# Hybrid decoder step on one core: the final sum and norm moved into the experts' block, with the sample tile on GpSimd

## The reference

```python
f = hier_moe(u, ...)                 # each token: gate0 * expert_a(u) + gate1 * expert_b(u)
hp = hp + f[:B * S].reshape(B, S, D) # prompt rows, 256 x 2048
hs = hs + f[B * S:].reshape(DB, DS, D)  # sample rows, 8 x 2048
y_prompt = rms_norm(hp, norm_final_g)
y_sample = rms_norm(hs, norm_final_g)
# rms_norm(x, g) = x * rsqrt(mean(x * x) + 1e-6) * g, all in float32
```

## Time and profile before

| | |
|---|---|
| median of 3 runs | 1697.02 us (1693.51 to 1700.8) |
| the profiled execution's own time | 1693.25 us |
| its span, first to last instruction | 1691.5 us |
| busy: PE, DVE, ACT, GpSimd | 77%, 40%, 14%, 4% |
| mean granted clock of TensorE | 0.864 |
| mean rate of the DMAs | 341 GB/s |

### The profile page before, as it was taken

The page is one execution under the profiler, slowest core; times in us unless marked ns, Lnnn a source line. Parts: engine busy times, 40 slices in busy tenths (PEclk is TensorE's granted clock), DMA queues, the critical chain, the costliest instruction groups (busy, mean ns, idle before and its releaser), DMA issues. The chain is left out here.

```text
span 1691.5 us, 24894 instructions
## 1 busy us (share of the span) xinstructions
PE 1299.3 (77%) x7991; PEld 816.7 (48%) x7992; DVE 678.5 (40%) x4789; ACT 230.3 (14%) x447; POOL 60.7 (4%) x100
## 2 busy tenths in 40 slices
PE   5999487888697979379997676676777577876771
PEld 3777355555465756237774222443444344433431
DVE  3005875756575757677446950020010000000015
ACT  1011011301212203020002111010011001100101
POOL 1000000000000000010000000000001000000000
PEclk9999789998898989679998767687899878888995
DMA  8453899999989999999997999959999999999954
GB/s 269 90 191 141 286 389 394 398 398 391 354 335 398 370 398 356 373 362 335 362 359 298 408 389 364 404 226 384 395 360 396 393 377 383 357 389 392 393 222 156
DMA packets 201805, 576.59 MB, mean 341 GB/s; under 512 B 28529, under 2 KB 116898, under 8 KB 183618
## 3 DMA queue, kind: packets, MB, share of 16 engines
q1 hardware_dynamic: 122144, 507.85, 76.8%
q10 hardware_dynamic: 75122, 58.46, 10.8%
q0 software_dynamic: 4432, 9.05, 1.7%
HBM read 568.68 MB, written 17.77 MB: 347 GB/s over the span
## 5 line engine op out<-in xcount | busy, mean ns | idle before, releaser
L119 DVE CUSTOM_DVE_ANT_0 ws<-ws,xgT 128x128 f32<-128x128 f32 x2048 | 441.8, 282 | 68.2 <-DMA ws<-in_cache_fox_k 29.4
L1682 PE MATMUL bank<-ws,xgT 128*64 128x256 f32 x1024 | 264.2, 423 | 127.5 <-DMA ws<-in_w_expert_up 123.9
L800 PE MATMUL bank<-xn,ws 128*128 128x264 f32 x1024 | 266.1, 417 | 53.3 <-DMA ws<-in_w_in 53.3
L800 PEld LDWEIGHTS bank<-xn,ws 128*128 128x128 f32 x1024 | 204.0, 205 | 140.2 <-DMA ws<-in_w_in 61.0
L1682 PEld LDWEIGHTS bank<-ws,xgT 128*64 128x64 f32 x1024 | 154.2, 154 | 236.0 <-DMA ws<-in_w_expert_up 121.1
L1684 PE MATMUL bank<-ws,xgT 128*64 128x256 f32 x1024 | 264.1, 423 | 0.0
L785 PE MATMUL bank<-ws,PR 128*32 128x512 f32 x1024 | 155.4, 688 | 35.5 <-DMA ws<-in_cache_fox_v 28.5
L1839 DVE COPY gu<-bank 128x256 f32<-128x256 f32 x32 | 13.6, 425 | 412.6 <-PE bank L1684 412.6
L119 DVE DVE_READ_ACCUMULATOR2_ANT Z<- 128x1 f32 x2048 | 159.6, 78 | 0.0
L1684 PEld LDWEIGHTS bank<-ws,xgT 128*64 128x64 f32 x1024 | 154.1, 154 | 0.0
L1703 PE MATMUL bank<-ws,hT 128*32 128x512 f32 x1024 | 115.9, 605 | 12.7 <-ACT xgT L1757 12.5
(11 more groups left out here) (372 smaller groups left out, 954.7 us busy)
## 6 DMA issues: line engine op xcount, KB each, us to landing
ws<-in_cache_sb_k SPq DMA_DIRECT2D x128, 512.0 KB, 8.2
ws<-in_cache_fox_k SPq DMA_DIRECT2D x128, 512.0 KB, 10.0
ws<-in_cache_sb_v SPq DMA_DIRECT2D x128, 512.0 KB, 7.2
ws<-in_cache_fox_v SPq DMA_DIRECT2D x128, 512.0 KB, 10.2
ws<-in_w_expert_gate SPq DMA_DIRECT2D x32, 2048.0 KB, 15.4
ws<-in_w_expert_up SPq DMA_DIRECT2D x32, 2048.0 KB, 17.3
ws<-in_w_expert_down SPq DMA_DIRECT2D x32, 2048.0 KB, 20.0
ws<-in_w_in ACTq DMA_DIRECT2D x16, 2048.0 KB, 31.7
```

The source lines that it names most:

```text
L119: ins = dve.tensor_tensor_reduce(k, k, qb[:, (g * H + h) * HD:(g * H + h + 1) * HD], 1.0, 0.0, ALU.mult, ALU.add, Z[:, n % 2, g, h, t:t + 1])
L800: mm = pe.matmul(out[:, 0:T], w[:, c, m * P:(m + 1) * P], xn[:, c, :], start=(c == 0), stop=(c == KC - 1))
L1682: pe.matmul(bank[2 * k][0:SLOTS, 0:256], lhs, ws[:, wg, c * 256:(c + 1) * 256], start=(c == 0), stop=(c == KC - 1))
```

## The change

The second block is gone; its instructions stand behind the experts' in the same block. What differs beside the place:

- GpSimd loads the five register values before the pairs instead of after them, and signals `all` when the last scatter has landed and the five branches are behind it. SP waits for `all`, then issues the six loads in the same order. It stores the tiles in the order 0, 2, 1.
- PE turns the residual rows in the last pair, between `gate_up(0)` and `gate_up(1)` (`token_rows`), through banks 4 to 7, and waits for all twelve copies before `down(0)`. ACT copies the banks to SBUF (`hrow`, which lies in `qo` and `xn`), before the last pair's Silu.
- The sample tile (2) is summed and normed on GpSimd, in single operations of 8x2048: `tensor_scalar` and `tensor_tensor` where DVE had one fused operation. Its reciprocal alone is on DVE, its square and root on ACT.
- DVE has the two prompt tiles, with one 128x2048 operation where there were four of 128x512, and its first addend comes from SBUF, not from a bank. Its order is add 0, add 1, reciprocal of tile 2, norm 0, norm 1. ACT's order is tile 2, 0, 1.

The diff, cut to its core; the second block's old text is left out, since it stands above:

```diff
+    hrow = [qo[:, :, :].rearrange("p c t -> p (c t)")[:, t * D:(t + 1) * D] for t in range(2)]
+    hrow.append(xn[:, :, :].rearrange("p c t -> p (c t)")[:, D:2 * D])
...
         @block.sync
...
             extra_pairs(sp, pair)
+            sp.wait_ge(F["all"], 1)
+            for t in (2, 0, 1):
+                lo, n = TILES[t]
+                for k in range(2):
+                    sp.dma_start(yr[0:n, t, k, :], y_rows[k * T + lo:k * T + lo + n, :]).then_inc(F[f"g{t}{k}"], 16)
+            for t in (0, 2, 1):
+                lo, n = TILES[t]
+                sp.wait_ge(F[f"out{t}"], 1)
+                dst = y_prompt[0, lo:lo + n] if t < 2 else y_sample.rearrange("b s d -> (b s) d")
+                sp.dma_start(dst, hr[0:n, t, :]).then_inc(F["st"], 16)
+            sp.wait_ge(F["st"], 48)
...
         @block.gpsimd
...
+            used = [in_use(pool, 2 * i) for i in range(PAIRS - EXP_PAIRS)]
             pool.wait_ge(E["dst"], 1)
...
             for n in range(EXP_PAIRS, PAIRS):
-                with pool.If(in_use(pool, 2 * (n - EXP_PAIRS)) > 0):
+                with pool.If(used[n - EXP_PAIRS] > 0):
...
+            pool.memset(pad[:, 7:8], 0.0).then_inc(F["all"], 1)
+            own = Steps(pool, F["pool"])
+            out, y0, y1 = hr[0:NB, 2, :], yr[0:NB, 2, 0, :], yr[0:NB, 2, 1, :]
+            pool.wait_ge(F["hc"], 12)
+            pool.wait_ge(F["g20"], 16)
+            own.step(pool.tensor_scalar(y0, y0, gates[0:NB, 2, 0:1], None, ALU.mult))
+            own.step(pool.tensor_tensor(out, y0, hrow[2][0:NB, :], ALU.add))
+            pool.wait_ge(F["g21"], 16)
+            own.step(pool.tensor_scalar(y1, y1, gates[0:NB, 2, 1:2], None, ALU.mult))
+            pool.tensor_tensor(out, out, y1, ALU.add).then_inc(F["sum2"], 1)
+            pool.wait_ge(F["sq2"], 1)
+            pool.tensor_scalar(rms[0:NB, 2:3], ssq[0:NB, 2:3], 1.0 / D, EPS, ALU.mult, ALU.add).then_inc(F["ms2"], 1)
+            pool.wait_ge(E["gf"], 16)
+            own.step(pool.tensor_tensor(out, out, gf[0:NB, :], ALU.mult))
+            pool.wait_ge(F["rec2"], 1)
+            pool.tensor_scalar(out, out, ssq[0:NB, 2:3], None, ALU.mult).then_inc(F["out2"], 1)
...
         @block.tensor
...
+            def token_rows():
+                pe.wait_ge(E["yc0"], 2 * EXP_PAIRS - 2)
+                pe.wait_ge(E["yc1"], 2 * EXP_PAIRS - 2)
+                for i in range(12):
+                    lo, n = TILES[i // 4]
+                    if i >= 4:
+                        pe.wait_ge(F["hc"], i - 3)
+                    for c in range(4):
+                        mm = pe.transpose(bank[4 + i % 4][0:n, c * P:(c + 1) * P], xT[:, 4 * (i % 4) + c, lo:lo + n], ident[:, :])
+                    mm.then_inc(F["hp"], 1)
...
-            def pair(n, ahead, first=False):
+            def pair(n, ahead, first=False, last=False):
                 pe.wait_ge(E["xgT"], 4 * n + 4)
                 gate_up(0, n)
+                if last:
+                    token_rows()
...
+                if last:
+                    pe.wait_ge(F["hc"], 12)
                 down(0, n)
                 down(1, n)
...
         @block.scalar
...
+            def token_rows():
+                for i in range(12):
+                    t, k = divmod(i, 4)
+                    n = TILES[t][1]
+                    act.wait_ge(F["hp"], i + 1)
+                    nc.scalar.activation(hrow[t][0:n, k * 512:(k + 1) * 512], bank[4 + k][0:n, :], ACT.Copy).then_inc(F["hc"], 1)
...
+            def pair(n, ahead, last=False):
+                if last:
+                    token_rows()
                 silu(0, n)
...
+            for t in (2, 0, 1):
+                n = TILES[t][1]
+                act.wait_ge(F[f"sum{t}"], 1)
+                if t != 2:
+                    act.wait_ge(F["sq2" if t == 0 else "sq0"], 1)
+                nc.scalar.activation(junk[0:n, :], hr[0:n, t, :], ACT.Square, accum_out=ssq[0:n, t:t + 1]).then_inc(F[f"sq{t}"], 1)
+                act.wait_ge(F[f"ms{t}"], 1)
+                nc.scalar.activation(rms[0:n, t:t + 1], rms[0:n, t:t + 1], ACT.Sqrt).then_inc(F[f"sqrt{t}"], 1)
...
         @block.vector
...
+            def add(t):
+                dve.wait_ge(F[f"g{t}0"], 16)
+                dve.wait_ge(F["hc"], 4 * t + 4)
+                fin.step(dve.scalar_tensor_tensor(out=hr[:, t, :], in0=yr[:, t, 0, :], scalar=gates[:, t, 0:1],
+                                                  in1=hrow[t], op0=ALU.mult, op1=ALU.add))
+                dve.wait_ge(F[f"g{t}1"], 16)
+                dve.scalar_tensor_tensor(out=hr[:, t, :], in0=yr[:, t, 1, :], scalar=gates[:, t, 1:2],
+                                         in1=hr[:, t, :], op0=ALU.mult, op1=ALU.add).then_inc(F[f"sum{t}"], 1)
...
+            add(0)
+            add(1)
+            dve.wait_ge(F["sqrt2"], 1)
+            dve.reciprocal(ssq[0:NB, 2:3], rms[0:NB, 2:3]).then_inc(F["rec2"], 1)
+            norm(0)
+            norm(1)
```

More of the change, by code:

```diff
@@ L521, in hybrid_step @@
         bctx.close()
-        experts(nc, ctx, ws, W, a, ident, iota, gcol, lastq, xT, xn, xgT, xg, wr, br, bank, sem, E, idx, dest, gates, extra,
+        experts(nc, ctx, ws, W, a, ident, iota, gcol, lastq, xT, xn, qo, xgT, xg, wr, br, bank, sem, E, idx, dest, gates, extra,
                 many, many2, destc, drow, sqs, srs, y_prompt, y_sample, u_rows, y_rows)
@@ L1554, in attention_and_route, with experts @@
         bstack.close()
-def experts(nc, ctx, ws, W, a, ident, iota, gcol, lastq, xT, xn, xgT, xg, wr, br, bank, sem, E, idx, dest, gates, extra,
+def experts(nc, ctx, ws, W, a, ident, iota, gcol, lastq, xT, xn, qo, xgT, xg, wr, br, bank, sem, E, idx, dest, gates, extra,
             many, many2, destc, drow, sqs, srs, y_prompt, y_sample, u_rows, y_rows):
@@ L1563, in experts @@
     gf = sb("gf", [P, D])
+    ssq = sb("ssq", [P, 3])
+    rms = sb("rms", [P, 3])
     dctx = ExitStack()
@@ L1579, in experts @@
     EXP_PAIRS = NE // 2
+    hrow = [qo[:, :, :].rearrange("p c t -> p (c t)")[:, t * D:(t + 1) * D] for t in range(2)]
+    hrow.append(xn[:, :, :].rearrange("p c t -> p (c t)")[:, D:2 * D])
+    rows = ws[:, :, :].rearrange("p s (a d) -> p (s a) d", d=D)
+    hr = rows[:, 0:3, :]
+    yr = rows[:, 3:9, :].rearrange("p (t k) d -> p t k d", k=2)
+    junk = rows[:, 9, :]
+    F = {n: sem("e_" + n) for n in ("hp hc all g20 g21 g00 g01 g10 g11 sum0 sum1 sum2 sq0 sq1 sq2 ms0 ms1 ms2 "
+                                    "sqrt0 sqrt1 sqrt2 rec2 out0 out1 out2 st dve pool").split()}
     def in_use(eng, i):
@@ L1747, in _ @@
                 pair(n, True)
-            pair(EXP_PAIRS - 1, False)
+            pair(EXP_PAIRS - 1, False, last=True)
             extra_pairs(pe, lone_pair)
@@ L1765, in silu @@
                 nc.scalar.activation(si[k][:, :, :], gv[:, :, 0:SLOTS], ACT.Silu).then_inc(E[f"si{k}"], 1)
-            def pair(n, ahead):
+            def token_rows():
[7 more added lines that the diff above has]
+                    token_rows()
                 silu(0, n)
@@ L1786, in _ @@
                 pair(n, True)
-            pair(EXP_PAIRS - 1, False)
+            pair(EXP_PAIRS - 1, False, True)
             extra_pairs(act, lone_pair)
+            for t in (2, 0, 1):
[6 more added lines that the diff above has]
+                nc.scalar.activation(rms[0:n, t:t + 1], rms[0:n, t:t + 1], ACT.Sqrt).then_inc(F[f"sqrt{t}"], 1)
         @block.vector
@@ L1855, in _ @@
             extra_pairs(dve, pair)
-    dctx.close()
[L1859 to L1941, removed]
@@ new lines, in _ @@
+            fin = Steps(dve, F["dve"])
+            def add(t):
[6 more added lines that the diff above has]
+                                         in1=hr[:, t, :], op0=ALU.mult, op1=ALU.add).then_inc(F[f"sum{t}"], 1)
@@ new lines, in norm @@
+            def norm(t):
+                dve.wait_ge(F[f"sq{t}"], 1)
+                dve.tensor_scalar(rms[:, t:t + 1], ssq[:, t:t + 1], 1.0 / D, EPS, ALU.mult, ALU.add).then_inc(F[f"ms{t}"], 1)
+                dve.wait_ge(F[f"sqrt{t}"], 1)
+                fin.step(dve.reciprocal(ssq[:, t:t + 1], rms[:, t:t + 1]))
+                dve.wait_ge(E["gf"], 16)
+                dve.scalar_tensor_tensor(out=hr[:, t, :], in0=hr[:, t, :], scalar=ssq[:, t:t + 1],
+                                         in1=gf[:, :], op0=ALU.mult, op1=ALU.mult).then_inc(F[f"out{t}"], 1)
```

## The result

The change made the kernel slower by a little: 1699.13 us in the median (20 runs, 1694.48 to 1704.36) against 1693.26 us for the kernel before (20 runs, 1685.04 to 1700.8) measured beside it. The medians differ by 5.9 us; the ratio is 1.0036 [1.0024, 1.0048], which is 4.1 to 8.1 us. Predicted were +2.6 us, 1695.8 us on the profiled execution; that execution of after took 1699.14 us, span 1697.4 us. The range held the result, but the loss is 5.9 us in place of 2.6.

What follows compares the result with a forecast made beforehand. The bound was DVE's 23.7 us tail after the first load, plus 4.3 us for the last store. Loads 6.95 us earlier, but GpSimd-DVE waits move DVE's end from 1687.2 to 1689.8: 1693.25 + 2.6 = 1695.8 us, range 1685.5 to 1704.

Steps and rivals of the forecast that it cites:

- The front: Before the tail's loads: one block drops drain and barrier, register loads move early; first load issues 6.95 us earlier.
- Rival E: Before the tail's loads: the 3.83 us drain stands ahead of `all` too; 1699.6 us, chance 0.06.
- The rows in the last pair: Residual transposes and copies fit under PE's 9.21 us wait for the up weights; effect zero, 5.1 us if uncovered.
- The clock: At gate_up(1) of the last pair: PE kept warm would save 1.45 us; taken as 0, kept for the range.
- The exclusion: In the tail: GpSimd operations reading SBUF and DVE products with two SBUF inputs each wait for the whole other.
- A: Main case, tail: GpSimd and DVE exclude each other; +2.6 us, 1695.8 us, chance 0.46.
- B: Rival, tail: same GpSimd durations, but side by side with DVE; -4.7 us, 1688.5 us, chance 0.27.
- The tensor_tensor: GpSimd's 8x2048 add in the sample tile takes 4.90 us, one input at cast pace, the second at memset pace.
- tensor_scalar: 0.33 + 1.72 = 2.05 to 0.33 + 2.85 = 3.18 ... so I take 2.05: GpSimd's 2048-column scale in the sample tile, from memset and cast paces; taken at the lower end, 2.05 us.
- Rival D: Tail: GpSimd at the cast's pace, 3.18 and 6.03 us, excluding DVE; +9.4 us, 1702.6 us, chance 0.11.
- the prediction's chain through ACT, the gain and norms 0 and 1: Tail after the sample's sum at 1674.4: ACT's squares and roots, GpSimd's gf product, DVE's norms, to 1689.8.
- the prediction's lower end for the gain: Before the tail's loads: gain 3.83 us less if GpSimd has the drain's delay anyway after its last indirect transfer.

Runs made afterwards that it cites:

- experiment 8: Changed kernel with sample tile back on DVE, its norm and store last, and register loads again behind the last scatter; one execution 1689.72 us against 1692.21 before.
- experiment 3: Kernel before, plus six GpSimd operations on spare data at the start of the experts' block, where GpSimd is free; one execution, 1692.75 us.
- experiment 5: Kernel before, plus six GpSimd 8x2048 sums on spare data in its second block, nobody waiting for them; one execution, 1705.63 us.
- experiment 2: Changed kernel with the sample tile's final sum and norm left out, its output rows zero; 1681.74 us, ratio 0.9949.
- experiment 4: Changed kernel with GpSimd's scales written as tensor_tensor, the factor broadcast over the columns; 1696.85 us, ratio 1.0038.

## Why the prediction came out as it did

**The front: right.** Predicted 6.95 us, measured 6.77; both of its halves stand in experiment 8. Rival E, the drain ahead of `all` too, is out.

**The rows in the last pair: right at zero.** PE's transposes run from 1618.75 to 1624.2 and ACT's copies to 1625.3, under the wait for the up weights, which ends at 1627.93. From the last pair's `gate_up(0)` to the memset of `pad` the trace has 38.56 us before and 38.68 after. The clock was not kept: gate_up(1) again starts at 0.50, as in the earlier trace rows, after 3.73 us in which PE did nothing. One stage of after (us, PE, PEld, DVE, ACT and POOL busy, granted clock, DMA share, GB/s):

```profile
1628.00:1630.90 2.90, 2.90 (x14) 1.85 (x16) 0.00 (x0) 0.00 (x0) 0.00 (x0) 0.50 0.89 373
```

**The exclusion: right**, and it was the choice between A and B: experiments 3 and 5 show it from both sides, with 8 partitions. The Trainium skill's sentence (SBUF — State Buffer, SBUF: two separate sides) that this is an exclusive lock, taken for the whole instruction, agrees with these rows for the adds. For a tensor_scalar it does not: DVE's product ran in its last 1.9 us.

**The tensor_tensor: nearly right.** Taken at 4.90 us, it is 4.50 alone in experiment 3; the Trainium skill's 4497 ns (GPSIMD Engine Reference, Elementwise — side-by-side cycle accounting) is that number.

**The step that failed is "tensor_scalar: 0.33 + 1.72 = 2.05 to 0.33 + 2.85 = 3.18 ... so I take 2.05".** It is 5.45 us, outside both ends, and was drawn from a memset and a cast: neither does arithmetic with a factor, and the ends were one kind of guess twice, not bounds. The working had one input cheaper than two; here the tensor_scalar with its one tensor (5.45) is dearer than the add of two (4.50), though a copy of one is cheap (1.90). Why is open. Against the predicted steps, from the first load:

| step | predicted | measured |
|---|---|---|
| GpSimd's start | 2.9 | 3.19 |
| scale y0 | 2.05 | 5.45 |
| add | 4.90 | 4.68 |
| DVE product, then scale y1 | 2.2 + 1.8 | 7.36, of which 1.9 wait |
| DVE product | 2.2 | none: beside the scale's end |
| add | 4.7 | 4.68 |
| sum of the sample | 20.8 | 25.6 |
| DVE's last end | 36.2 | 40.4 |

The scales' excess of 2 x 3.4 us came back in part, 2.2 us, since a DVE product fits beside the end of a tensor_scalar; with the small differences of the other rows 4.8 us are left at the sample's sum. From there the prediction's chain through ACT, the gain and norms 0 and 1 took 14.8 us against 15.4, in the order that it names; the last scale (7.35 us, from 1684.16) held DVE's norm 1 for 2.8 us. The span's end comes 5.4 us after DVE's, not 4.3: the stores of the sample and of tile 1 are ready within 0.4 us, where the prediction had 2.9 and more. Whether that is its cause stays open, since experiment 2 has 5.28 us with its last store 2.9 us behind the one before, and experiment 4 has 4.29 with 2.1 us between its last two. So +2.6 became 2.6 + 0.2 + 4.2 + 1.1 = 8.1 us in these two traces. Rival D, +9.4, came nearest to these traces, and that is luck: it made the adds dear (6.03), which they are not, and the scales 3.18.

**Two points on the sum itself.** Its terms are smaller than the sizes stated for them: a product of 2.35 us is put in as 2.2 and the second and third scale of 2.05 as 1.8, without a reason. With the stated sizes and 0.1 us a handover the same chain ends at about 1692.5, which is +5.3: nearer to the result, and for the wrong reason. The traces bear out the 2.2: a product held by an add ended 2.15 us behind it (1677.17 to 1679.32). And 1699.6 us, the sum on the median of three runs, lies 0.5 us from the 1699.13 measured only because that median was 3.8 us above the one of 20 runs, while the loss was 3.3 us too small.

## What to carry to other kernels

Before work is given to GpSimd to relieve DVE, ask what DVE reads meanwhile: beside GpSimd arithmetic, products with both inputs in SBUF stop, and those with a bank as an input don't. Ask also who waits for GpSimd's result: here ACT's queue did, and the prompt tiles behind it. Both together made 18.5 us of a sample tile that was 4.0 us on DVE. An operation that the trace doesn't have is not bounded by cheaper kinds of operation; its range must reach at least to the dearest operation whose price is known, and what the kernel's time would be is worked out at that end too. What paid here, in the traces: no block boundary ahead of a chain of loads and register values loaded early (6.8 us), DVE's longer operations with the new order (0.9), and the smallest store last (1.4), which together take 9.1 us off the tail.

## What the runs showed that was not expected

- On GpSimd, 2048 columns of f32: tensor_scalar 5.45 us, tensor_tensor 4.50 and copy 1.90 (experiment 3), tensor_tensor with a broadcast factor 3.59 (experiment 4), memset 1.79 (experiment 2) to 1.81. The number of partitions changes nothing (5.45 and 5.48).
- A tensor_scalar of 5.45 us holds DVE's products for 3.4 to 3.6 us of them, a tensor_tensor to its end. Waits go both ways: beside DVE products of 2.35 us, a tensor_tensor reads up to 6.45 (experiment 5).
- One row does not fit "both inputs in SBUF": in experiment 3 a DVE tensor_scalar of 40x4 with a single tensor in SBUF, which takes 0.16 us in the kernel before, read 0.68 us from 1113.36 and ended with GpSimd's tensor_scalar of 8x1024 (1111.18 + 2.83 = 1114.01), although a tensor_tensor with both inputs in SBUF had just run at full pace beside it (0.15 us at 1113.18). What holds a single-input operation stays open.
- GpSimd's drain at the end of the experts' block outlasts its last instruction by 3.8 to 3.95 us, whether that was a branch, a memset or a scale. In after it starts beside the last scale (1684.16 + 7.35 = 1691.5) and ends 3.9 us behind it, at 1695.4; the last scatter had landed by 1650.37. So it is no rest of a transfer, as the prediction's lower end for the gain had it. It ends before the last store is waited for (SP goes on at 1697.0) and costs nothing there. The block of experiment 5 that has only the adds ends with a drain of 0.04 us; what the 3.9 us hang on stays open. The rows of GpSimd's sequencer, first after's, then that of experiment 5's last block (ns min/median/max, first and last start):

```profile
L1602 POOLq DRAIN  x1: 11267/11267/11267, 1684.1 to 1684.1; - x1
```

```profile
L1869 POOLq DRAIN  x1: 38/38/38, 1694.7 to 1694.7; - x1
```
